# A decoder block on one core: a root moved behind a block, low parts first, squares by tile, a narrower bank wait

## The reference

```python
h = rmsnorm(x, g1);  z = h @ w_in                      # 12 x 1024 columns
branches = rglru(z), hgrn2(z), conformer_conv(z)       # three token mixers
x = x + rmsnorm(sum(sigmoid(gates) * (branches @ w_branch)) @ w_mix_out, g2)
mem_n = rmsnorm(mem, gm);  k, v = split(mem_n @ wkv)   # 256 memory tokens
p = softmax((rmsnorm(x, g3) @ wq) @ k.T / 16)          # 4 heads of 256
x = x + rmsnorm((p @ v) @ wo, g4)
h = rmsnorm(x, g5)
x = x + rmsnorm(square(relu(h @ w1)) @ w2, g6)         # hidden width 4096
```

## Time and profile before

| | |
|---|---|
| median of 3 runs | 2566.24 us (2564.16 to 2569.15) |
| the profiled execution | 2562.92 us, span 2561.1 us |
| mean granted clock of PE | 0.991 |
| PE busy | 2497.6 us, 98% |
| DVE, POOL, ACT busy | 1532.2 us (60%), 1224.8 us (48%), 576.2 us (22%) |
| chain that ended last | PE 84%, DVE 7%, issue 3%, ACT 2%, POOL 2% |

### The profile page before, as it was taken

One profiled execution on the slowest core, in us unless ns is written; L12 is line 12 of the kernel. 1 busy time (PEld: TensorE's weight loads), 2 busy tenths in 40 slices (PEclk: granted clock), 3 DMA queues, 4 the chain that ended last, 5 costly groups with the idle time before them and its releaser, 6 DMA issues.

```text
span 2561.1 us, 31052 instructions
## 1 busy us (share of the span) xinstructions
PE 2497.6 (98%) x11450; PEld 2058.0 (80%) x11450; DVE 1532.2 (60%) x1660; ACT 576.2 (22%) x761; POOL 1224.8 (48%) x941
## 2 busy tenths in 40 slices
PE   8999999999999999999999999989989999999996
PEld 5788888788888888888778887778778888888885
DVE  6696577677778777699666737572861321622123
ACT  4110444322222222111111214253431110111000
POOL 0333333322222233333777777715766666766663
PEclk9999999999999999999999999999999999999998
DMA  6322121211111113332744445512533222423323
GB/s 231 126 74 75 65 82 57 73 36 47 41 47 43 41 57 108 114 132 109 263 178 148 142 137 166 185 61 68 171 99 99 95 94 98 162 93 98 99 98 107
DMA packets 84882, 270.10 MB, mean 105 GB/s; under 512 B 7888, under 2 KB 9168, under 8 KB 83792
## 3 DMA queue, kind: packets, MB, share of 16 engines
q1 hardware_dynamic: 71760, 244.03, 27.9%
q10 hardware_dynamic: 13056, 25.17, 2.8%
HBM read 224.60 MB, written 44.56 MB: 105 GB/s over the span
## 4 chain that ended last, share of the span: by engine, by line
PE 84%; DVE 7%; issue 3%; ACT 2%; POOL 2%; DMA 1%; SPq 0%; ACTq 0%; POOLq 0%; DVEq 0%
PE ps L367 25%; PE ps L369 25%; PE ps L368 25%; PE xb L505 2%; PE ps L431 1%; POOL w_lo L1888 1%; PE ps L421 1%; DVE macc L757 1%; DMA w_raw<-wall 1%; POOL w_hi L1886 1%; DVE cdev L763 1%; ACT yb_hi L1494 1%; PE xb L528 1%; PE xa L541 1%; PE xb L531 0%
## 5 line engine op out<-in xcount | busy, mean ns | idle before, releaser
L1888 POOL TENSOR_TENSOR w_lo<-w_raw,w_hi 128x1024 fp32r<-128x1024 f32 x312 | 792.4, 2540 | 26.0
L1885 POOL TENSOR_TENSOR small<-small 128x1 f32<-128x1 f32 x312 | 89.3, 286 | 1280.7 <-PE ps L369 1081.1
L367 PE MATMUL ps<-h_hi,w_hi 128*128 128x512 f32 x1408 | 559.3, 397 | 2.0 <-issue 1.8
L369 PE MATMUL ps<-h_hi,w_lo 128*128 128x512 f32 x1408 | 548.7, 390 | 0.0
L368 PE MATMUL ps<-h_lo,w_hi 128*128 128x512 f32 x1408 | 548.4, 389 | 0.0
L367 PE MATMUL ps<-yb_hi,w_hi 128*128 128x512 f32 x1024 | 404.1, 395 | 11.6 <-POOL w_lo L1888 9.1
L368 PE MATMUL ps<-yb_lo,w_hi 128*128 128x512 f32 x1024 | 400.5, 391 | 0.0
L369 PE MATMUL ps<-yb_hi,w_lo 128*128 128x512 f32 x1024 | 400.1, 391 | 0.0
L1886 POOL TENSOR_SCALAR w_hi<-w_raw 128x1024 fp32r<-128x1024 f32 x312 | 355.3, 1139 | 0.0
L367 PEld LDWEIGHTS ps<-h_hi,w_hi 128*128 128x128 f32 x1408 | 264.8, 188 | 56.9 <-issue 5.1
L369 PEld LDWEIGHTS ps<-h_hi,w_lo 128*128 128x128 f32 x1408 | 264.2, 188 | 55.7
(11 more groups left out here) (270 smaller groups left out, 2859.6 us busy)
## 6 DMA issues: line engine op xcount, KB each, us to landing
w_raw<-wall SPq DMA_DIRECT2D x312, 512.0 KB, 3.5
gst<-gate_d SPq DMA_DIRECT2D x24, 512.0 KB, 4.5
w_kv<-wall SPq DMA_DIRECT2D x16, 512.0 KB, 3.9
x_d<-xx ACTq DMA_DIRECT2D x16, 512.0 KB, 3.1
gate_d<-sigb SPq DMA_DIRECT2D x12, 512.0 KB, 2.6
gate_d<-gbuf SPq DMA_DIRECT2D x12, 512.0 KB, 2.8
xs_xa<-x_d ACTq DMA_DIRECT2D x12, 512.0 KB, 5.1
x_sb<-xT SPq DMA_DIRECT2D x2, 2048.0 KB, 15.2
```

What stands on the lines that cost most here:

```text
L367: nc.tensor.matmul(out, wh, xh, start=start, stop=False)
L369: return nc.tensor.matmul(out, wl, xh, start=False, stop=stop)
L1885: nc.gpsimd.tensor_tensor(small[:, 13:14], small[:, 12:13], small[:, 12:13], ALU.add)
L1888: nc.gpsimd.tensor_tensor(w_lo[:, u], w_raw[:, u], w_hi[:, u].bitcast(F32), ALU.subtract).then_inc(w_split, 1)
```

## The change

It has four parts:
1. At the start, the first value tile stands ahead of the ones matmul of x. The first conformer tile does its first half behind the weights and `evac[0] >= 6`, and `take(8, 0)` stands between its two halves.
2. The root of `chain(3)` that ends up 0 of the first half stands behind up 1, on PE, ACT and DVE alike.
3. In attention, `pt_lo` stands ahead of all four statistics, and `value_low(i, 1)` behind all four divisions.
4. In down 3, ACT squares one tile at a time (the first straight into the PSUM sum), DVE adds the square of tile t - 1 behind the eviction of tile t, and the square of the last tile is added by PE: a second ones matmul into the same bank, for both `post_stat(4)` and `post_stat(5)`.

```diff
 # PE
             for n in range(1, KB):
                 keys_tile(n)
+            values_tile(KB)
             pe.wait_ge(xacc_done, KB)
...
-            for n in range(KB, 2 * KB):
+            for n in range(KB + 1, 2 * KB):
                 values_tile(n)
...
                 if first(i):
-                    take(m, 0)
+                    pe.wait_ge(w_split, 1)
+                    pe.wait_ge(evac[0], KB // 2 + 2)
                     for k in range(KB):
                         pe.wait_ge(h_split, k + 1)
                         mm3(ps[0][:, 0:HALF], w_hi[:, 0, k], w_lo[:, 0, k], h_hi[:, k, 0:HALF], h_lo[:, k, 0:HALF], k == 0, k == KB - 1)
+                    take(m, 0)
                     half_of(0, 1).then_inc(mm_done, 1)
...
                 pe.wait_ge(nacc_ready[h], q)
-                nc.tensor.matmul(stat[h], ones[:], nacc[h][:], start=True, stop=True).then_inc(nstat_done[h], 1)
+                if c < 4:
+                    nc.tensor.matmul(stat[h], ones[:], nacc[h][:], start=True, stop=True).then_inc(nstat_done[h], 1)
+                    return
+                nc.tensor.matmul(stat[h], ones[:], nacc[h][:], start=True, stop=False)
+                pe.wait_ge(ysq_done, KB * (h + 1))
+                nc.tensor.matmul(stat[h], ones[:], sqm[:, 1], start=False, stop=True).then_inc(nstat_done[h], 1)
...
-                if c is not None and c < 4:
+                if c is not None and c < 3:
                     pre_stat(c)
...
                     elif kind == "up":
                         half_tiles(n0 // 2, yb_hi[h], yb_lo[h])
+                        if h == 0 and b == 1:
+                            pre_stat(3)
 # DVE
                 pair(3)
-                root(c, q + 1)
+                if c < 3:
+                    root(c, q + 1)
...
                 more = i + 2 < 2 * XA_HEADS
-                if more:
-                    softmax_stat(i + 2, 0)
                 dve.wait_ge(pt_hi_done, i + 1)
                 low(pt_lo[:], xa[:].rearrange("p (m n) -> p m n", m=MT), pt_hi[:]).then_inc(pt_split, 1)
                 if more:
-                    for st in range(1, ST):
+                    for st in range(ST):
                         softmax_stat(i + 2, st)
-                for dt in range(2):
-                    value_low(i, dt)
-                    if more:
-                        for st in range(2 * dt, 2 * dt + 2):
-                            softmax_div(i + 2, st)
+                value_low(i, 0)
+                if more:
+                    for st in range(ST):
+                        softmax_div(i + 2, st)
+                value_low(i, 1)
...
+            def last_sum(h, t):
+
+                if t < 1:
+                    return
+                dve.wait_ge(ysq_done, KB * h + t + 1)
+                if t > 1:
+                    dve.wait_ge(ysum_done, (KB - 2) * h + t - 1)
+                ins = add(sums[h] if t < KB - 2 else nacc[h][:], sums[h], sqm[:, t % 2])
+                ins.then_inc(ysum_done, 1)
+                if t == KB - 2:
+                    dve.wait_ge(ysum_done, (KB - 2) * (h + 1))
+                    dve.sem_inc(nacc_ready[h], 1)
...
+                        if h == 0 and b == 1:
+                            root(3, 4)
...
-                        for j in range(KB // 2):
-                            down_out(m0 + j, h, j, j % 2)
-
-                            dve.wait_ge(ysq_done, 4 * h + j + 1)
-                            if j == 0:
-                                done(add(sums[h], sqm[:, 0], sqm[:, 1]))
-                            else:
-                                done(add(sums[h], sums[h], sqm[:, 0]))
-                                ins = add(sums[h] if j < 3 else nacc[h][:], sums[h], sqm[:, 1])
...
+                        for t in range(KB):
+                            down_tile(m0 + t // 2, h, t // 2, t // 2 % 2, t % 2)
+                            last_sum(h, t - 1)
 # ACT
                 pair(3)
-                norm_root(c, q + 1)
+                if c < 3:
+                    norm_root(c, q + 1)
...
+                        if h == 0 and b == 1:
+                            norm_root(3, 4)
...
-                        for j in range(4):
-                            for u in range(2):
-                                act.wait_ge(evac[u], m0 + j + 1)
-                            a.activation(sqm[:], xx[h][:, 2 * j:2 * j + 2], ACT.Square).then_inc(ysq_done, 1)
+                        for t in range(KB):
+                            act.wait_ge(evac[t % 2], m0 + t // 2 + 1)
+                            if t > 2:
+                                act.wait_ge(ysum_done, (KB - 2) * h + t - 2)
+                            a.activation(sqm[:, t % 2] if t else sums[h], xx[h][:, t], ACT.Square).then_inc(ysq_done, 1)
```

More of the change, by code:

```diff
@@ L347, in build @@
                              "pv_done", "o_hi_done", "o_split"))
-        ffsq_done, ff_hi_done, ff_split, ysq_done = (sem(s) for s in ("ffsq_done", "ff_hi_done", "ff_split", "ysq_done"))
+        ffsq_done, ff_hi_done, ff_split, ysq_done, ysum_done = (sem(s) for s in ("ffsq_done", "ff_hi_done", "ff_split", "ysq_done", "ysum_done"))
         out_stored = sem("out_stored")
@@ L1440, in wait_sum, with down_tile @@
                     dve.wait_ge(evac[u], m)
+            def down_tile(m, h, j, r, u):
+                t = bass.ds(2 * j + u, 1)
+                dve.wait_ge(mm_done, 2 * m + u + 1)
+                add(xx[h][:, t], xx[h][:, t], half_bank(u, r)).then_inc(evac[u], 1)
             def down_out(m, h, j, r):
                 for u in range(2):
-                    t = bass.ds(2 * j + u, 1)
-                    dve.wait_ge(mm_done, 2 * m + u + 1)
-                    add(xx[h][:, t], xx[h][:, t], half_bank(u, r)).then_inc(evac[u], 1)
+                    down_tile(m, h, j, r, u)
+            def last_sum(h, t):
[9 more added lines that the diff above has]
+                    dve.sem_inc(nacc_ready[h], 1)
             for h in range(2):
```

## The result

The changed kernel took 2550.39 us, the median of six runs (2548.27 to 2552.06); beside it the kernel before took 2564.33 (2562.66 to 2569.15). The forecast was 2550.8. The profiled execution took 2550.88 with a span of 2549.1, 12.0 less than before, at a mean clock of 0.994 instead of 0.991. PE is busy for 2495.8 us, still 98%; DVE, ACT and POOL are where they were (1535.0, 576.5, 1225.4).

A forecast was written before the change was run, and what follows sets the result against it. PE, busy 98% of the span, bounds the kernel, so only its waits and slow-clock stretches can be won. 4.6 + 8.8 + 0.8 + 1.2 = 15.4 us off the 2566.2 median forecast 2550.8, range 2546 to 2557.

The forecast's parts named there:

- Part 2: MLP: moving the root behind the second block removes PE's 7.56 us wait and slow clock; 8.8 us net gain.
- The 0.4 allowed for pair 1 of the second block: MLP second block: a 0.4 us loss allowed for pair 1 waiting on DVE's eviction of pair 3 and POOL's next split.
- rival 2: MLP second block: DVE's low parts stand behind POOL's splits; part 2 gives 6.6 or less, sum 9 to 11 us; 8%.
- Part 3: Attention: pt_lo comes once earlier, with no shorter head cycle; 0.8 us gain.
- the ring: Attention: DVE and ACT's repeating cycle of 7.86 us a head, including 1.27 idle, claimed to keep its length when permuted.
- upper bound of 4.6: Attention: the most the reordering was taken to give, 4.6 us, if all later gaps for pt_lo went.
- Part 4: Last squares: 2.1 us gained behind the last product, 0.9 lost in the first half's root; 1.2 us net.
- part 1: Start: values' first tile fills PE's wait for the x squares, clock kept, projection wait shortened; 4.6 us gain.
- the thinnest cover: Start: PE's third tile needs ACT's first sigmoid, behind the store of keys and values; 0.6 us of slack left.
- An idle of 1.95 us is nearer to the 1.77 that kept the clock than to the 3.17 that lost it.: Start, first value tile: the clock is taken as kept, worth 1.7 us; if it falls, the start gives 2.9.
- The stores perhaps 1.8: Start: stores of keys and values, issued behind POOL's second split, come perhaps 1.8 us earlier while PE comes 4.6 earlier.
- rival 1: Start: third tile behind the stores, or clock lost; part 1 gives 2.9, sum 11 to 13.5, 2554 us; 15%.

The follow-up runs named there:

- part 1 alone: The kernel before with only the start's change (first value tile ahead of the ones matmul, first projection tile split): 2561.01 us, ratio 0.999.
- the changed kernel once more: The changed kernel measured again without edits, on a chip shared with other runs: 2548.82 us, ratio 0.9929 to the kernel before.
- divisions first: The changed kernel, with DVE doing all four attention divisions of head i + 2 ahead of both low parts of head i: 2544.45 us, ratio 0.9916.
- early stores: The changed kernel, with SP storing the two key arrays right behind the last key tile, before the projection's first weights: 2547.69 us, ratio 0.993.
- by k: The changed kernel, with the first tile of branch blocks 2 to 5 waiting for DVE's low part pair by pair of k: 2549.88 us, ratio 0.993.
- narrow bank: The changed kernel, with the first value tile waiting for evac >= 3 instead of 4 and the fifth for the rest: 2551.45 us, ratio 0.9942.
- both together: The changed kernel with the key arrays stored early and the first value tile's narrower bank wait: 2550.87 us, ratio 0.9935.
- three edits: The changed kernel with early key stores, the narrower bank wait and the attention divisions ahead of both low parts: 2544.94 us, ratio 0.9916.
- part 3 alone: The kernel before with only attention reordered, pt_lo ahead of all statistics and value_low(i, 1) behind all divisions: 2563.38 us, ratio 1.0003.
- the three edits with by k: The changed kernel with early key stores, narrower bank wait, divisions first and the branch wait by pairs of k: 2538.97 us, ratio 0.9891.

## Why the prediction was right, and where it was not

**Part 2 was right, in size and in mechanism.** Forecast 8.8; alone it gave 8.8. The wait behind the first block is 0.6, for DVE's eviction, as worked out. The 0.4 allowed for pair 1 of the second block was not needed. The mechanism of rival 2 did appear there; DVE's and POOL's timelines after:

```profile
1872.41 1.28 DVE L1419 SCALAR_TENSOR_TENSOR sqm<-ps,rn 128x512 f32<-128x512 f32 x2
...
1880.01 3.50 DVE L755 TENSOR_TENSOR hx_lo<-sqm,hx_hi 128x512 fp32r<-128x512 f32 x2
1883.43 1.28 DVE L1419 SCALAR_TENSOR_TENSOR sqm<-ps,rn 128x512 f32<-128x512 f32 x2
```

```profile
1880.26 2.70 POOL L1909 TENSOR_TENSOR w_lo<-w_raw,w_hi 128x1024 fp32r<-128x1024 f32 x1
```

Two low parts that take 1.3 us when undisturbed took 3.50 beside POOL's split, and the eviction behind them was half done at 1884.1, just when PE asked for the bank. The rival fell by a margin of a tenth or two, not by its mechanism. The Trainium skill's rule, cited in the prediction (SBUF — State Buffer, "Who interferes with whom"), agrees with these rows.

**Part 3 was right.** 0.7 of 0.8, and the statement that an edit which only permutes the ring keeps its length held: 7.86 before, 7.85 after. What the forecast did not see is that the idle inside the ring could be filled. The divisions need nothing of ACT's eviction, and moving them into it took away four waits of 0.87 to 1.09, 4.1 us in sum, and 5.4 us of PE's time, above the upper bound of 4.6.

**Part 4 was right.** The tail is 2.0 shorter (2.1 forecast). ACT's last square takes 0.63, from 2529.90, and PE's timeline shows the four records at full clock after 1.44 of idle:

```profile
2530.58 1.12 PE L633 MATMUL xa<-nacc,ones 128*128 128x512 f32 x2 [1.44 <-DVEq L1471]
2531.54 1.02 PE L635 MATMUL xa<-sqm,ones 128*128 128x512 f32 x2
```

**The step that failed is part 1.** Forecast 4.6, measured 1.0 in the profiled execution, 2.5 in part 1 alone and 2.8 in the changed kernel once more. Two statements of it were wrong; the first stood there as a lower bound, the second as the thinnest cover.

*"An idle of 1.95 us is nearer to the 1.77 that kept the clock than to the 3.17 that lost it."* The idle was 2.07 or 2.08, and it is in neither class: of the six profiled executions with this wait, three kept the clock (3.67 us for the eight records: part 1 alone, changed once more, divisions first) and three lost it (5.37: the changed kernel, early stores, by k). The 1.7 us is a draw: with early stores and in the changed kernel once more PE restarted at the same 40.42, after 2.08 and 2.07 us, and lost the clock in the one and kept it in the other. The bracket of 1.77 and 3.17 was also wider than the trace of before: there PE waited 2.56 us near 505 us and ran at the low clock behind it. The Trainium skill (TensorE: Matmul & The Clock Gate, "What's actually happening") says of the slow stretch at a kernel's start that "it's run-variable". Here it varies between executions whether such a stretch comes at all behind the same wait.

*"The stores perhaps 1.8"* earlier, with 0.6 of slack left for the third tile. This was the cover that broke. The stores are issued behind POOL's second split, and the forecast moved that split earlier as a thing of fixed length. DVE's and POOL's timelines after:

```profile
66.30 4.66 DVE L755 TENSOR_TENSOR h_lo<-ht,h_hi 128x1024 fp32r<-128x1024 f32 x2
...
73.41 3.21 DVE L755 TENSOR_TENSOR h_lo<-ht,h_hi 128x1024 fp32r<-128x1024 f32 x2
```

```profile
65.57 1.04 POOL L1907 TENSOR_SCALAR w_hi<-w_raw 128x1024 fp32r<-128x1024 f32 x1
66.69 3.19 POOL L1909 TENSOR_TENSOR w_lo<-w_raw,w_hi 128x1024 fp32r<-128x1024 f32 x1
72.25 1.28 POOL L1906 TENSOR_TENSOR small<-small 128x1 f32<-128x1 f32 x1 [2.36 <-PE ps L431]
73.50 2.06 POOL L1907 TENSOR_SCALAR w_hi<-w_raw 128x1024 fp32r<-128x1024 f32 x1
75.64 3.25 POOL L1909 TENSOR_TENSOR w_lo<-w_raw,w_hi 128x1024 fp32r<-128x1024 f32 x1
```

Before, POOL's first split (65.88 to 72.38) met DVE's last two low parts, and its second ran alone, from 72.72 to 76.40. Now the root of x is later and the first split earlier. The first split meets the low parts before the last two, which take 4.66 instead of 2.35, so the last two fall into the second split, which takes 72.25 to 78.89, 6.6 us instead of 3.7. SP issued the stores at

```profile
79.35 3.58 SPq L1967 DMA_DIRECT2D kv_d<-kv  x4
```

where it had issued them at 76.86: 2.5 later, not 1.8 earlier. With part 1 alone, where the clock was kept, the low parts and the splits have the same durations within 0.01 us, and the stores were issued at 77.65, still 0.8 later. The sigmoid ended at 95.65 instead of 93.13, and PE, 2.3 earlier (96.5 to 94.21), waited 1.49. The experiment with early stores takes just this wait away and returns 1.5 us. With the clock kept as well, part 1 would have been 2.8 + 1.5 = 4.3, near the forecast's 4.6; that combination was in no run. Part of the rest lies in the projection's first two tiles, which take 22.7 us (71.53 to 94.21) where they had taken 22.2.

So rival 1 came true in both of its halves, which the forecast had called unlikely together. Its 2.9 is the price of one half; by the forecast's own terms both leave 4.6 - 1.7 - 1.7 = 1.2, and 1.0 was measured. (Rival 2's total has a slip that changed nothing here: with the 6.6 in part 2 the sum is 4.6 + 6.6 + 0 + 1.2 = 12.4, and its 9 to 11 needs 3.2 to 5.2 there, which no row gives.) The sum of 15.4 compares with 12.0 between the spans: 3.6 are part 1's, 0.7 the late keys, 0.2 attention and up 0, and parts 2 and 4 gave back 0.5 (10.45 instead of 10.0), the stretch from 504 to 1449 us 0.6 that no step had claimed: it is the wait for POOL's split near 1230 us. Between the medians it is 13.9: the profiled execution of the kernel before (2562.92) lies 1.4 under its median beside the result, that of the changed kernel 0.5 above its own. The gain was thus 1.5 under the forecast's. That the median still fell on the forecast is luck: the kernel before, on whose 2566.24 the forecast stands, took 2564.33 beside the result, 1.9 less.

## What to carry to other kernels

When an edit moves two engines against each other, go through the pairs of instructions that newly overlap, not only through the moved one: a split priced at 3.7 us became 6.6 because another engine's work slid under it, and a store behind it turned a slack of 0.6 into a wait. In the ring of two engines that wait for each other, permuting members left the length as it was; what shortened it was work that needs neither side, put into the idle (7.85 to 6.50 us per head). When gains at the start fail to arrive at the end, look for a later place with two outcomes, and make the wait there tolerant before adding up medians.

## What the runs showed that was not expected

**A race with two outcomes.** Near 1443 us DVE ends a pair of low parts and goes on to a pair of products, `yst`, when POOL begins a split. In the changed kernel's profiled execution DVE came first. DVE's and POOL's timelines:

```profile
1442.21 1.28 DVE L755 TENSOR_TENSOR hx_lo<-macc,hx_hi 128x512 fp32r<-128x512 f32 x2
1443.41 2.13 DVE L770 TENSOR_TENSOR yst<-cdev,crs 128x512 f32<-128x512 f32 x2
1447.51 1.37 DVE L755 TENSOR_TENSOR yb_lo<-yst,yb_hi 128x1024 fp32r<-128x1024 f32 x1 [1.98 <-ACT yb_hi L1511]
```

```profile
1442.79 0.75 POOL L1906 TENSOR_TENSOR small<-small 128x1 f32<-128x1 f32 x1 [1.05 <-PE ps L369]
```

With part 1 alone POOL came first:

```profile
1441.93 1.31 DVE L748 TENSOR_TENSOR hx_lo<-macc,hx_hi 128x512 fp32r<-128x512 f32 x2
1443.16 4.33 DVE L763 TENSOR_TENSOR yst<-cdev,crs 128x512 f32<-128x512 f32 x2
1449.46 3.25 DVE L748 TENSOR_TENSOR yb_lo<-yst,yb_hi 128x1024 fp32r<-128x1024 f32 x1 [1.97 <-ACT yb_hi L1497]
```

```profile
1442.50 0.19 POOL L1888 TENSOR_TENSOR small<-small 128x1 f32<-128x1 f32 x1 [1.05 <-PE ps L369]
```

```profile
1453.09 0.79 PE L367 MATMUL ps<-yb_hi,w_hi 128*128 128x512 f32 x1 [5.23 <-DVE yb_lo L748]
```

POOL's small instruction starts 0.58 us behind DVE's low parts in the good case (1442.21 to 1442.79) and 0.57 in the bad one (1441.93 to 1442.50). In the good case it takes 0.75 beside DVE's low parts; in the bad one 0.19, and DVE is the one that is late beside the split behind it: 4.33 instead of 2.13, then 3.25 instead of 1.37. PE waits 5.23 instead of 1.08 and restarts at the low clock, about 7 us in all. Of the profiled executions, those of part 1 alone, the narrow bank, both together, divisions first and by k (where it cost little) had the bad outcome. It fits the gaps in the lists of times: the kernel before has 3 of 30 runs above 2571 on one chip and 7 of 11 above 2568 on another. The mean granted clock fits too: in these two lists it is 0.988 to 0.990 in the ten long runs and 0.990 to 0.993 in the others, and in three edits 0.993 or 0.994 in the four long ones against 0.995 in the two shortest. That these are the same thing is inferred, since only profiled executions show the place. The best evidence is that the median of three edits fell by 6.0 us and its spread from 10.5 to 2.2 once the first tile waits by k; but the changed kernel once more had a spread of 1.8 without that edit, and some of the times of three edits lie between the two outcomes, so another source of scatter is not excluded.

**The clock after a short idle.** In all 14 profiled executions PE kept 1.00 after idles of up to 1.77 us, and ran at the low clock behind every idle of 2.7 and more (such as 2.72 and 2.82). In between it went either way: 2.07 or 2.08 at the first value tile (three kept, three lost), and 2.52 to 2.57 at the wait for `hg_attn` near 505 us, where four kept it (part 1 alone, part 3 alone, narrow bank, and the three edits with by k) and ten lost it. PE's timelines at the latter, in the changed kernel and with part 1 alone:

```profile
506.79 3.44 PE L508 MATMUL xb<-hg_qp,hg_kp 128*128 128x128 f32 x16 [2.52 <-DVE hg_attn L1117]
```

```profile
505.29 2.02 PE L508 MATMUL xb<-hg_qp,hg_kp 128*128 128x128 f32 x16 [2.55 <-DVE hg_attn L1110]
```

What a lost clock costs depends on what follows. Here the kept clock saves 1.4 us at once, but in just the four executions that kept it PE then waits 0.9 for DVE some 17 us later, and the stretch up to the wait near 1230 us takes 719.2 instead of 719.5 to 719.7.
